# Depthwise convolution of a two-layer block: products on ScalarE, wide additions on VectorE, half-summed layer norm, and a last product split by token tile over four steps

## What is computed

```python
def conformer_conv(u, b_glu, w_dw, b_dw, ln_g, ln_b):
    u = u + b_glu
    val, gt = jnp.split(u, 2, axis=-1)
    h = val * jax.nn.sigmoid(gt)
    # 31 causal taps, each channel by itself
    y = depthwise_conv(h, w_dw, padding=[(30, 0)])
    y = layer_norm(y + b_dw, ln_g, ln_b)      # mean and variance over the 1024 channels
    return jax.nn.silu(y)

mixed = jnp.concatenate([attn, conv], axis=-1) @ w_out
```

## Time and profile before

| | us |
|---|---|
| median of 3 runs | 1823.86 |
| lowest, highest | 1823.67, 1825.38 |
| span of the profiled execution | 1822.8 |
| TensorE busy in it | 1803.1 (99%) |
| VectorE busy | 1468.4 (81%) |
| ScalarE busy | 902.7 (50%) |
| GpSimd busy | 112.4 (6%) |

### The profile page before, as it was taken

How to read it: one execution, slowest core, us unless ns; L and a number is a source line. 1 busy time by engine, 2 the same in 40 slices (tenths; PEclk the granted TensorE clock), 3 DMA queues, 4 the chain that set the end, 5 groups by cost and what they waited for, 6 DMA issues and landing times.

```text
span 1822.8 us, 26157 instructions
## 1 busy us (share of the span) xinstructions
PE 1803.1 (99%) x9898; PEld 1560.7 (86%) x9898; DVE 1468.4 (81%) x1704; ACT 902.7 (50%) x1176; POOL 112.4 (6%) x217
## 2 busy tenths in 40 slices
PE   8999999999999999999999999999999999999998
PEld 7899988888888888888888888888888888888986
DVE  6899998878888897889887788755788778897854
ACT  6444566555335533553354557423656545445453
POOL 0000000000000000000000000001111010001000
PEclk9999999999999999999999999999999999999999
DMA  9756448777786787778977865654665784878562
GB/s 326 256 175 199 153 157 301 263 242 256 265 289 226 264 292 231 247 260 287 248 255 270 313 213 163 230 184 149 221 211 203 273 294 137 277 242 282 191 227 97
DMA packets 191017, 426.93 MB, mean 234 GB/s; under 512 B 12480, under 2 KB 12864, under 8 KB 189760
## 3 DMA queue, kind: packets, MB, share of 16 engines
q1 hardware_dynamic: 158560, 323.74, 52.3%
q0 software_dynamic: 27648, 100.68, 16.6%
q10 hardware_dynamic: 4704, 1.07, 0.3%
HBM read 421.23 MB, written 4.21 MB: 233 GB/s over the span
## 4 chain that ended last, share of the span: by engine, by line
PE 94%; DVE 3%; ACT 1%; issue 1%; DMA 1%; DVEq 0%; POOLq 0%; ACTq 0%
PE banks L2064 23%; PE banks L2109 14%; PE banks L2110 14%; PE banks L2111 14%; PE banks L2070 12%; PE banks L2055 4%; PE banks L2057 4%; PE banks L2056 4%; PE banks L2415 2%; PE banks L2431 2%; PE banks L2172 1%; PE banks L2406 1%; ACT w_hi L548 0%; DVE w_lo L1144 0%; DMA mod_raw<-in_ev_mod_w 0%
## 5 line engine op out<-in xcount | busy, mean ns | idle before, releaser
L548 ACT ACTIVATE w_hi<-raw 128x1024 fp32r<-128x1024 f32 x552 | 579.5, 1058 | 659.3 <-PE banks L2111 334.6
L1144 DVE TENSOR_TENSOR w_lo<-raw,w_hi 128x1024 fp32r<-128x1024 f32 x552 | 666.9, 1222 | 242.5 <-ACT w_hi L548 240.5
L2064 PE MATMUL banks<-a_pair,w_hi 128*128 128x512 f32 x1792 | 431.2, 391 | 1.6 <-DVE a_pair L1246 0.9
L2064 PEld LDWEIGHTS banks<-a_pair,w_hi 128*128 128x128 f32 x1792 | 328.3, 188 | 65.3 <-issue 2.2
L2109 PE MATMUL banks<-w_hi,b_hi 128*128 128x512 f32 x808 | 316.2, 391 | 0.2 <-DVE b_lo L1409 0.2
L2111 PE MATMUL banks<-w_hi,b_lo 128*128 128x512 f32 x808 | 314.5, 389 | 0.0
L2110 PE MATMUL banks<-w_lo,b_hi 128*128 128x512 f32 x808 | 314.4, 389 | 0.0
L1184 DVE SCALAR_TENSOR_TENSOR mod_sum<-mod_raw,silu_c,mod_sum 128x1024 f32<-128x1024 f32 x240 | 302.9, 1283 | 11.3 <-DMA mod_raw<-in_ev_mod_w 7.6
L2070 PEld LDWEIGHTS banks<-a_pair,w_lo 128*128 128x128 f32 x1792 | 230.2, 191 | 8.7
L2070 PE MATMUL banks<-a_pair,w_lo 128*128 128x256 f32 x1792 | 234.6, 283 | 0.0
L2109 PEld LDWEIGHTS banks<-w_hi,b_hi 128*128 128x128 f32 x808 | 151.7, 188 | 31.9 <-DVE b_lo L1409 0.6
(11 more groups left out here) (246 smaller groups left out, 1680.7 us busy)
## 6 DMA issues: line engine op xcount, KB each, us to landing
raw<-in_w_ff SPq DMA_DIRECT2D x128, 1024.0 KB, 6.6
mod_raw<-in_ev_mod_w POOLq DMA_DIRECT2D x96, 512.0 KB, 5.4
mod_raw<-in_od_mod_w POOLq DMA_DIRECT2D x96, 512.0 KB, 5.3
raw<-in_ev_w_in SPq DMA_DIRECT2D x40, 1024.0 KB, 5.2
raw<-in_w_in SPq DMA_DIRECT2D x39, 1024.0 KB, 5.2
raw<-in_od_w_in SPq DMA_DIRECT2D x32, 1024.0 KB, 5.8
raw<-in_w_out SPq DMA_DIRECT2D x16, 1024.0 KB, 6.3
raw<-in_ev_w_out SPq DMA_DIRECT2D x16, 1024.0 KB, 6.7
```

The costliest lines, as they stand in the source:

```text
L548: nc.scalar.activation(w_hi[:, s % SLOTS], raw[:, s // 2, KPS * (s % 2):KPS * (s % 2) + KPS, :], ACT.Copy).then_inc(hi_ready, 1)
L1144: nc.vector.tensor_tensor(w_lo[:, s % SLOTS], raw[:, s // 2, KPS * (s % 2):KPS * (s % 2) + KPS, :], w_hi[:, s % SLOTS].bitcast(F32), ALU.s ...
L2064: e = nc.tensor.matmul(out[:, f, :], w_hi[:, s % SLOTS, t, P * f:P * (f + 1)], rows[:, :, KPS * s + t, :], start=s == 0 and t == 0, stop=F ...
```

## The change

Of the 31 taps of a channel tile, ScalarE now multiplies the first 14 for four tiles at a time: `tap_group` is four ACTIVATEs on 128x256 into one of the two buffers of `mod_raw`. VectorE adds such a product 1024 wide (`conv_sum`), 13 times for each four tiles. The other 17 taps of each tile stay as they were, 136 instructions instead of 248. Semaphores `conv_product` and `conv_wide` pass the buffers: a group waits for the wide addition that freed its buffer, an addition waits for its product. A group stands between the two roundings of each pair of steps on ScalarE.

```diff
+def groups_at(point):
+    return min(point + (2 if point == 0 else 3 if point <= WIDES else 4), QUADS * ACT_TAPS)
...
             pool.wait_ge(split_done, 8 + 4)
             first_loads("ev_gate", "ev", 2)
-            load_mod("ev_gate", "ev", 2, 1, KT)
+            load_mod("ev_gate", "ev", 2, 1, 4)
+            pool.wait_ge(conv_wide, QUADS * WIDES)
+            load_mod("ev_gate", "ev", 2, 4, KT)
...
+            def tap_group():
+                n = product_now[0]
+                q, t = n // ACT_TAPS, n % ACT_TAPS
+                if t == 0:
+                    act.wait_ge(acc_free, 2 + ACC["u"] + 2 * q + 2)
+                if n < 2:
+                    act.wait_ge(mod_acc, MOD_STEP0["ev_gate"] + 8)
+                else:
+                    act.wait_ge(conv_wide, WIDES * ((n - 2) // ACT_TAPS) + max((n - 2) % ACT_TAPS, 1))
+                for c in range(4):
+                    ct = 4 * q + c
+                    dst, src, w = tap_products[n % 2][:, c, :], conv_in[:, ct, t:t + T], col("w_dw", TAPS * ct + t)
+                    if t == 0:
+                        e = nc.scalar.activation(dst, src, ACT.Identity, bias=col("b_dw", ct), scale=w)
+                    else:
+                        e = nc.scalar.activation(dst, src, ACT.Copy, scale=w)
+                e.then_inc(conv_product, 1)
...
+            def conv_sum():
+                q, w = divmod(wide_now[0], WIDES)
+                y = conv_y[:, 4 * q:4 * q + 4, :]
+                dve.wait_ge(conv_product, ACT_TAPS * q + w + 2)
...
+                nc.vector.tensor_tensor(y, y if w else tap_products[(n - 1) % 2], tap_products[n % 2], ALU.add).then_inc(conv_wide, 1)
...
+            def conv_ahead(b, point):
+                for m in range(4):
+                    ahead, s = b + (m >= 2), (2 * m + 4) % STEPS
+                    split_lo(ahead, [s])
+                    if 0 < point + m != WIDES:
+                        conv_sum()
+                    split_lo(ahead, [s + 1])
+                    if point + m in (0, WIDES):
+                        if point:
+                            conv_taps(quad_taps - tap_now[0])
+                        conv_sum()
+                    conv_taps(2 if point + m == WIDES else 5)
```

```diff
+            def channels_added(src, done):
+                link(nc.vector.tensor_tensor(conv_half, src[:, 0:4, :], src[:, 4:8, :], ALU.add))
+                link(nc.vector.tensor_tensor(conv_half[:, 0:2, :], conv_half[:, 0:2, :], conv_half[:, 2:4, :], ALU.add))
+                nc.vector.tensor_tensor(ln_rstd[:], conv_half[:, 0, :], conv_half[:, 1, :], ALU.add).then_inc(done, 1)
...
-            nc.vector.tensor_reduce(ln_rstd[:], conv_y.rearrange("p c t -> p t c"), AX.X, ALU.add).then_inc(conv_total, 1)
...
-            halves("ev_gate", 8, 2)
+            dve.wait_ge(conv_sq_ready, 1)
+            channels_added(conv_sq, square_total)
...
-            halves("ev_gate", 10, 1)
+            halves("ev_gate", 8, 3)
...
-            out_step(6)
-            out_step(7)
-            pe.wait_ge(conv_sq_ready, 1)
+            for n in range(6, 9):
+                out_step(n)
+            pe.wait_ge(square_total, 1)
             pe.wait_ge(head_copied, HEADS)
-            channel_sums(ln_var, conv_sq)
-            for n in range(8, 30):
+            nc.tensor.matmul(ln_var, ones[:], ln_rstd[:], start=True, stop=True).then_inc(ln_sum, 1)
+            for n in range(9, 30):
                 out_step(n)
```

```diff
-            add_to_residual(range(3), [0])
+            add_to_residual(range(NBLK), [0])
             gained(2 * (3 * NBLK - 1), NBLK - 1, acc[1], None, [1])
             dve.wait_ge(acc_free, 2 + ACC["odo"] + 4)
             post_scale("odo", 1)
-            add_to_residual([0], [1])
-            add_to_residual([3], [0])
-            add_to_residual(range(1, NBLK), [1])
+            add_to_residual(range(NBLK), [1])
...
-                product(BLOCK["odo"] + n, ACC["odo"] + n, acc[n % 2], step_tokens, a_hi, a_lo, p_ready, FT, 0, by_tile=n == 3)
+                product(BLOCK["odo"] + n, ACC["odo"] + n, acc[n % 2], step_tokens, a_hi, a_lo, p_ready, FT, 0, by_tile=4 * (n == 3))
```

118 lines of the change are left out of this document (80 added, 38 removed).

## The result

The changed kernel takes **1838.1 us** (median of 4, 1837.2 to 1838.7) against 1823.8 us before: ratio 1.0077, 95% interval 1.0062 to 1.0091. It is 0.8% slower, as forecast (1837.9 us). Its profiled span is 1836.9 us, 14.1 more than before.

The account below looks back on a forecast made before the run. TensorE, busy 1803.1 of 1822.8 us, was taken as the bound, with little slack for VectorE's splits. 1822.8 + 5.0 + 7.2 + 2.5 - 0.7 = 1836.8, plus 1.1 from span to median: 1837.9 us, range 1827.5 to 1843.

Parts of the forecast that it names:

- part 1: Convolution with products on ScalarE: VectorE's splits come late for TensorE at u3.4, q0.4, q3.4; +5.0 us, bounds 3.5 and 6.5.
- parts 2 and 3: Layer norm sums and half 10's load together: o16 starts +7.2 us later than before; low bound +2.3.
- part 4: TensorE's rate behind the wait at o16: slow matmuls at half rate, +2.5 us, bounds 0 and 5.
- part 5: The end: four residual additions behind the last matmul instead of five, tile 0's lying beside tile 1; -0.7 us.
- the small waits of part 1 cost only themselves: TensorE's waits at u3.4, q0.4 and q3.4, 1 to 2 us each, bring no half rate behind them.
- Part 2: Layer norm's sum of squares: 14 of 16 passes go, -3.0 us; +1.6 us given back at o12 for `b_lo`.
- Part 3: Behind the layer norm: half 10's load, issued after half 8's use, lands 9.0 us later; 8.5 us wait at o16.
- A: Rival: ScalarE keeps pace, VectorE stays within its slack and part 1 is nil; 1832.9 us, chance 0.20.
- B: Rival: half 10's load takes about 4.1 us, parts 2 and 3 are +2.3, the rate holds; 1830.5 us, chance 0.15.
- C: Rival: saved matmuls are the only effect, half 10 early enough, VectorE never late; 1820.0 or 1821.6 us, chance 0.10.
- The remark on the later halves: Loads of halves 12 to 19, median 6.5 us, come at most 0.5 us late for the last steps.

Follow-up runs that it names:

- e5_spread_late: The changed kernel with 3 taps in the first four split pairs, 4 in later ones, the last 12 spread over three head slots; 1832.9 us, ratio 1.0049.
- e11_first_four: The changed kernel with 3 taps instead of 5 in the first four pairs of splits only, leftover taps in head slots; 1834.6 us, ratio 1.0056.
- e1_use_early: The changed kernel with modulation halves 8 and 9 ahead of the wait for the mean's sums, only half 10 behind the layer norm; 1828.7 us, ratio 1.0024.
- e9_early_loads: e5_spread_late with halves 8 and 9 in head slots 4 and 5, 10 and 11 ahead of the mean, later halves two places earlier; 1823.7 us, ratio 0.9997.
- e7_sums_only: The kernel before with the new layer norm sums, and halves 8 and 9 ahead of the wait for the mean; 1825.4 us, ratio 1.0007.
- e12_best: e5_spread_late, halves 8 and 9 before the mean, two-part multiplication, steps 37 to 39 one feature later, halves 10 and 11 back to back; 1826.8 us.
- e3_keep_busy: The changed kernel with 34 unused products keeping TensorE at work ahead of its wait at output step 16; 1836.7 us, ratio 1.0070.
- e10_two_parts: e9_early_loads with the multiplication by the inverse deviation in two parts and step 11's split between them; 1823.3 us, ratio 0.9995.

## Why the prediction was right, point by point

The measured sum, in the prediction's own order: start +0.2, part 1 +5.1, parts 2 and 3 +8.0, part 4 +1.8, part 5 -1.1. That is 14.0 against the 14.1 us of the spans. Forecast were 5.0, 7.2, 2.5 and -0.7. The mechanisms were right in the main, but that the totals agree to 0.2 us is luck: parts 2 and 3 came 0.8 us dearer, part 4 came 0.7 cheaper and part 5 gave 0.4 more.

- **Part 1, right in sum and in VectorE's times.** With the start of 0.2 us taken off, VectorE was 2.4 us late at the sum for the sigmoid (forecast 2.2), 4.0 at the split of q0.4 (3.8) and 5.9 at the softmax (5.9). The first addition came at 74.13 (73.6): 0.2 us of that is the start, the rest is the first group, which took 2.08 us instead of 1.7. e5_spread_late shows that VectorE's order is the cause, and e11_first_four that 3.6 us of it go with shorter pairs at the start.
- **Part 1, wrong in what TensorE does between.** The forecast had waits at u3.4, q0.4 and q3.4; q0.4 has none. That "the small waits of part 1 cost only themselves" failed: behind 1.9 us at u3.4 come 1.7 us at a granted clock of 0.57. It cost nothing in the sum only because VectorE was the bound up to q0.4. In e1_use_early the clock held behind a wait of 2.1 us there, and the 1.5 us were lost at q0.4 instead, behind a wait of 1.3 us: q1.0 is 4.1 us late in both.
- **Part 2, close in both sizes, wrong in place.** The 14 passes that went are 2.9 us (3.0): step o8 comes 3.3 us earlier, but the two passes that are left, 0.4 us, now stand behind it. Given back are 1.8 us (1.6), 1.5 of them at o11, for the split queued behind the multiplication, and not at o12 for `b_lo`; 1.0 us is kept up to o15. It is kept without part 1's delay too (e5_spread_late 1.0, e9_early_loads 1.0). e7_sums_only, with two modulation steps ahead of the mean, keeps 0.2 of it, and e12_best, with the chain to the low parts put in another order, 2.1. So the variance's cost has moved from TensorE's queue to VectorE's, and the order there decides what is kept.
- **Part 3, right in mechanism and place, mis-sized by a little.** The wait is 8.9 us (8.5), the load took 9.6 us (9.0, taken from half 12's in before).
- **Part 4, right, mis-sized.** 1.8 us against 2.5; e3_keep_busy took 1.7 of it away. The start of the program, from which the 2.5 came, was too high a guide.
- **Part 5, right.** 1.1 us against 0.7; the last stores on ScalarE's queue are shorter too.
- **Rivals.** Of A (ScalarE keeps pace) the half is true: it does, but VectorE does not. B (the load lands early) is out: wherever VectorE waited 2 us or more for a half between 300 and 320 us, it came 8.3 to 10.4 us after its issue. C needed halves 8 and 9 used early; e1_use_early did it and still ended 0.24% above before, since part 1 and a later load stood in the way. e9_early_loads and e10_two_parts come closer to C's conditions (they lose 1.3 us in the head slots, and no load reaches TensorE) and end level with before, because 1.8 to 1.9 of the 2.9 us saved are given back to VectorE's chain.
- **The remark on the later halves**, "at most 0.5 us late for the last steps", held in after, where VectorE's long wait stood ahead of them. In the profiled executions of e1_use_early and e7_sums_only the same loads cost 3.4 and 1.6 us there.

## What to carry to other kernels

- An engine with 19% of its time free may still have none at the place where it counts. Before work is taken from it on average, look at how much slack each place has, and spread the work by that: with the same instructions, three taps instead of five in four places and four in sixteen others gave 5.2 us.
- A step that uses up a buffer also issues the next load. Where such a step is moved, write down when the buffer's next load is issued and what stands in the queue behind the step that waits for it; moving two steps of 1.2 us behind the layer norm cost 9.6 us.
- Matmuls that are saved ahead of a chain on other engines are worth only what that chain allows. Ask which chain ends next (here variance, reciprocal, multiplication, split), and shorten it first.
